# Shared value projection: eight quarter-size block products become seven, with sums of weight blocks and of activation blocks made beside them

## The chip, the cores and the metric

The kernel runs on one core of a Trainium2 chip. The metric is the device time of one execution in microseconds (us); the time before is 1315.62 us, the median of three runs (1315.57 to 1315.96).

## What is computed

The reference chains two small transformer blocks over 512 tokens of width 1024 in float32. The change touches one product in the first block, the shared values that every head of a later attention layer reads:

```python
if i == N_A - 1:
    kv = rmsnorm(x, kv_ln_g) @ w_kv_shared
    k_sh = kv[..., :MIX_WIDTH].reshape(B, S, N_HEADS, HEAD_DIM).transpose(0, 2, 1, 3)
    v_sh = kv[..., MIX_WIDTH:].reshape(B, S, N_HEADS, HEAD_DIM).transpose(0, 2, 1, 3)
```

Here `x` is 512 x 1024 and each half of `w_kv_shared` is 1024 x 1024. The keys' half is computed by the stage `sh_k`, the values' half by the stage `sh_v`.

## The kernel before

All programs of the five engines are written out by hand, one instruction list per engine; semaphores order them. The work is a list `LINEARS` of matrix products that TensorE walks one after the other. The stages that matter here are, in order, `gate0`, `sh_k`, `sh_v`, `sb_gate`.

Each product is made in float32 by splitting: every operand has a high part (rounded to `F32R`) and a low part (what is left), and each 128 x 128 by 128 x 512 product is three matmuls, high x high, high x low, low x high (`three`, L494 to L498). A weight matrix is read in **slabs** of two 128-row tiles by 512 columns (128 partitions x 1024 numbers, 512 KB):

- SyncE (SP) loads the slab into one of four `stage` buffers (`load`, L465), once VectorE has finished with the slab four places before (`lo_ready`);
- ScalarE (ACT) writes its high part to one of two `w_hi` buffers (`split` of ACT, L1108), once TensorE has finished with the slab two places before (`ring_used`);
- VectorE (DVE) writes the low part to `w_lo` (`split` of DVE, L1689), and that is what TensorE waits for (`lo_ready`).

One slab serves 24 matmuls: two k-tiles, four output tiles, three products each. A group of 512 output columns is four slabs and fills four of the eight PSUM banks; the next group uses the other four. A stage of 1024 columns is two groups, eight slabs, 192 matmuls.

While TensorE works on a stage, ACT and DVE do other things in between the slabs: `linear(name, read, extra)` walks the slabs in order; at each slab it first calls `split_to`, then reads finished banks, then pops one entry of the list `extra`. So an entry of `extra` stands behind the split of one slab and ahead of the split of the next on that engine. During `sh_k` the entries are the split of the next activations (`hi_two`, `lo_two`) and, on DVE, the RMS norm's tail (`norm`, L1770 to L1781).

The norm of this layer is finished inside `sh_k`: before its matmuls of k = 6, TensorE sums the squares over the tokens' features (`token_sums`, L592); DVE and POOL make the reciprocal root; at k = 7 TensorE spreads it (L605, `rstd_done`). `sh_k` multiplies it in when its banks are read (`kT_sh`, L1795). `sh_v` is computed with tokens on the partitions, so its banks are scaled by one number per partition (`nrm`) when ACT copies them to `v_sh` (L1194). POOL has nothing to do during `sh_v` except clearing two buffers.

The buffers: `stage`, `w_hi`, `w_lo` as above; `xT` holds the layer's input, `a0h`/`a0l` the high and low part of the gained activations, `s_...` and `sv_slot` appear only in the change.

Of the kernel before, what the change touches and what calls it, by code (L numbers as in the profile page):

```python
# [114 lines left out]
def build(nc, ctx, ins, out, cols):  # L115
# [90 lines left out]
    rope_b = [put(f"rope_b{s}", [P, MB, ROPE], 84.5 + 0.5 * s) for s in range(2)]  # L206

    kT_sh = put("kT_sh", [P, KD, T], 32)
    v_sh = put("v_sh", [P, MB, D], 48)
# [133 lines left out]
    def columns(a, b, step=T):  # L343
# [15 lines left out]
        Linear("sh_k", w_sh, 8, columns(0, D), False, A0, items("h_kv")),  # L359
        Linear("sh_v", w_sh, 8, columns(D, 2 * D), True, A0, items("h_kv")),  # L360
        Linear("sb_gate", w_sb, 8, columns(D, 2 * D), False, A1, items("h_sb")),
# [17 lines left out]
    read_by = {"out0a": ("src_ready", source(first_item["x0"]) - 1), "out0": ("src_ready", source(first_item["x0"]) + 3), "out1": ("src_ready", source(first_item["x1"]) - 1),  # L379
               "g_out": ("x_new", 24), "b_out": ("x_new", 32),  # L380
               "gate1": ("g_read", 0), "g_v": ("g_read", 8), "g_u": ("g_read", 24), "g_g": ("g_read", 40)}
    bank_free = {"mla_gate0": [("mla_cq_read", 4), ("src_ready", source(first_item["latent"] + 4))], "mla_gate1": [("mla_gate1_read", 7)] * 2}
    group_read = []
    for L in LINEARS:
        lin[L.name] = L
        L.load0, L.group0 = len(loads), n_groups
        L.read, L.read0 = read_by.get(L.name, (L.name + "_read", 0))
        for g, (c0, w) in enumerate(L.groups):
            group_read.append((L.read, L.read0 + 4 * (g + 1)))
            if L.by_tile:  # L390
                for c in range(c0, c0 + w, P):
                    loads.append((L, 0, L.kt, c, P))
            elif L.name == "out0a":
                loads.append((L, 0, 6, c0, P))
                for k0 in range(0, 6, 2):
                    loads.append((L, k0, 2, c0 + P, w - P))
                loads.append((L, 6, 2, c0, w))
                L.lpg = 5
            else:
                for k0 in range(0, L.kt, 2):  # L400
                    loads.append((L, k0, min(2, L.kt - k0), c0, w))
        n_groups += L.n
# [17 lines left out]
    def end_load(name):  # L420
        return lin[name].load0 + lin[name].lpg * lin[name].n

    def slab(t, L, nk, w):
# [5 lines left out]
    loaded = [S(f"loaded{s}") for s in range(4)]  # L429
    block = ctx.enter_context(nc.Block())  # L430
# [19 lines left out]
    def _(sp_):  # L450
# [3 lines left out]
        def load(r, i=None):  # L454
            L, k0, nk, c0, w = loads[r]
            src = L.w[k0 * P:(k0 + nk) * P, :].rearrange("(k p) n -> p k n", p=P)
            turn = 0 if i is None else i * (2 * L.lpg)
            if r >= 4:
                sp_.wait_ge(S("lo_ready"), turn + (r - 3))
# [5 lines left out]
            sp_.dma_start(slab(stage[r % 4], L, nk, w), src).then_inc(loaded[r % 4], 16)  # L465

        for r in range(end_load("proj0")):
            load(r)
        for m in range(MB):
            sp_.dma_start(x_tok[:, m, :], ins["x"][0, m * P:(m + 1) * P, :]).then_inc(S(f"x_in{m}"), 16)  # L470
        for L in LINEARS[1:]:
            if L.name in LOOPED:
                with sp_.Fori(0, L.n // 2) as i:
                    for r in range(L.load0, L.load0 + 2 * L.lpg):
                        load(r, i)
            else:
                for r in range(L.load0, end_load(L.name)):
# [15 lines left out]
    def _(pe):  # L493
# [130 lines left out]
        def x_columns(a, b):  # L624


            def do():
                if a == 0:
                    pe.wait_ge(S("gains_ok"), 2)
                    pe.wait_ge(S("act_lo"), 2)  # L630
                    for m in range(MB):
                        pe.wait_ge(S(f"x_in{m}"), 16)
                for k in range(a, b):
# [184 lines left out]
        linear("sh_k", 1)  # L818
        linear("sh_v")
        linear("sb_gate")  # L820
# [261 lines left out]
    def _(act):  # L1082
# [10 lines left out]
        def split(r, i=None):  # L1093
# [5 lines left out]
            if r == 0:  # L1099
# [4 lines left out]
                return  # L1104
            act.wait_ge(loaded[r % 4], 16 * (r // 4 + 1) + turn * 32)
            if r >= 2:
                act.wait_ge(S("ring_used"), r - 1 + turn * 8)
            act.activation(slab(w_hi[r % 2], L, nk, w), slab(stage[r % 4], L, nk, w), ACT.Copy).then_inc(S("hi_ready"), 1)  # L1108

# [359 lines left out]
        def sb_values(i, first=False):  # L1469
            if not first:  # L1470
                act.wait_ge(S("o2_done"), 2 * i)
            vs = v_sh[:, :, i * P:(i + 1) * P] if isinstance(i, int) else v_sh[:, :, bass.ds(i * P, P)]
            act.activation(v_pair2[:, :, :], vs, ACT.Copy).then_inc(S("v2_ok"), 1)
# [192 lines left out]
    def _(dve):  # L1666
# [10 lines left out]
        def split(r, i=None):  # L1677
# [4 lines left out]
            if r == 0:  # L1682
# [5 lines left out]
            dve.wait_ge(S("hi_ready"), r + 1 + (0 if i is None else 8 * i))  # L1688
            dve.tensor_tensor(slab(w_lo[r % 2], L, nk, w), slab(stage[r % 4], L, nk, w), slab(w_hi[r % 2], L, nk, w), ALU.subtract)\  # L1689
               .then_inc(S("lo_ready"), 1)  # L1690
# [18 lines left out]

        def linear(name, read=None, extra=(), then=None, first=None, further=False, near=False):  # L1710

# [12 lines left out]
            def groups(count, i=None):  # L1724
# [9 lines left out]
                if first:  # L1734
                    first()
                reads(count - 1, range(2), i)
                if further:
# [336 lines left out]
        rest_of_layer(0, 1, "h_kv")  # L2074
        linear("sh_k", normed_to(kT_sh, 1), [nothing, nothing, norm(1, 1e-6, "sh_k")] + [lo_two("h_sb", t) for t in range(4)])
        linear("sh_v")
        linear("sb_gate", normed_to(sg, 1))
# [290 lines left out]
    def _(pool):  # L2368
# [7 lines left out]

        pool.wait_ge(S("x_in3"), 16)
        for w, name in enumerate(("mla_q_head_g", "mla_k_head_g")):
# [101 lines left out]

        root(nrm, MB, "nrm_in", 2, "nrm_ok")
        pool.wait_ge(S("x_new"), 16)
        def kq_parts(pair, s, kq):
# [14 lines left out]

        pool.wait_ge(S("sh_k_read"), 8)
        def no_low(t, s):  # L2500

# [159 lines left out]
```

## Time and profile before

| what | value |
|---|---|
| median of three runs | 1315.62 us (1315.57 to 1315.96) |
| span of the profiled execution, first to last instruction | 1314.1 us |
| TensorE busy | 1295.6 us, 99% of the span |
| VectorE, ScalarE, GpSimd busy | 758.1, 642.3, 343.7 us |
| TensorE's share of the chain that ended last | 89% |
| `sh_v` on TensorE | 384.73 to 428.25 us |

The span is the part of an execution that the trace covers; the 1.5 us between it and the median lie around it and are not in the trace. The chain that ended last is followed back from the last instruction to what released each step, so an engine's share there is time that it, and not a wait, set.

### The profile page before, as it was taken

How to read it: one execution, taken by the hardware profiler on the slowest of the kernel's cores; microseconds unless marked ns; L12 is line 12 of the kernel's file. 1: busy time of each engine (PE TensorE's matmuls, PEld its weight loads, DVE VectorE, ACT ScalarE, POOL GpSimd, SP SyncE). 2: the span in 40 equal slices, each digit the busy share in tenths (PEclk: the TensorE clock that was granted, in tenths of full speed). 3: DMA queues.
4: the chain of work that ended last, by engine and by line, in shares of the span. 5: the costliest groups of instructions: out<-in, count | busy, mean ns of one | idle time of the engine just before them, and what ended most of it. 6: DMA issues, size and time to landing. Idle time of an engine off the chain costs nothing.

```text
span 1314.1 us, 17855 instructions
## 1 busy us (share of the span) xinstructions
PE 1295.6 (99%) x6478; PEld 1086.5 (83%) x6478; DVE 758.1 (58%) x1209; ACT 642.3 (49%) x1164; POOL 343.7 (26%) x393
## 2 busy tenths in 40 slices
PE   7999999999999999999999999999999999999998
PEld 6998778788888888888888888889888888888986
DVE  5656889735652226898444653335467335578843
ACT  5379888624432325998244433414234234355632
POOL 2238877400000007773000000000000000668620
PEclk9999999999999999999999999999999999999999
DMA  5332100132232232001323333332332421421121
GB/s 192 84 108 65 45 25 15 53 106 97 81 99 97 99 99 73 17 0 32 112 97 93 87 93 97 96 97 64 87 110 82 135 96 49 129 65 49 33 64 65
DMA packets 70867, 104.66 MB, mean 80 GB/s; under 512 B 3476, under 2 KB 31368, under 8 KB 70664
## 3 DMA queue, kind: packets, MB, share of 16 engines
q1 hardware_dynamic: 69584, 99.44, 24.3%
q0 software_dynamic: 1088, 4.17, 1.1%
q8 instruction: 47, 0.77, 0.2%
q14 instruction: 28, 0.23, 0.1%
q10 hardware_dynamic: 120, 0.05, 0.0%
HBM read 101.55 MB, written 2.10 MB: 79 GB/s over the span
## 4 chain that ended last, share of the span: by engine, by line
PE 89%; DVE 5%; issue 3%; ACT 2%; DMA 1%; SPq 0%; DVEq 0%; POOL 0%; ACTq 0%; POOLq 0%
PE ps L496 24%; PE ps L498 23%; PE ps L497 23%; PE ps L700 3%; PE ps L1006 2%; PE ps L858 2%; PE ps L713 1%; PE ps L950 1%; PE ps L679 1%; PE ps L727 1%; PE ps L848 1%; DVE sp L2086 1%; PE ps L849 1%; PE ps L728 1%; DVE sp_l L2091 1%
## 5 line engine op out<-in xcount | busy, mean ns | idle before, releaser
L1689 DVE TENSOR_TENSOR w_lo<-stage,w_hi 128x1024 fp32r<-128x1024 f32 (+4 forms) x188 | 224.1, 1192 | 415.1 <-ACT w_hi L1108 414.9
L1108 ACT ACTIVATE w_hi<-stage 128x1024 fp32r<-128x1024 f32 (+4 forms) x188 | 191.0, 1016 | 457.2 <-PE ps L498 456.8
L496 PE MATMUL ps<-a0h,w_hi 128*128 128x512 f32 x512 | 204.5, 399 | 1.1 <-DVE q_lo L2273 0.8
L498 PE MATMUL ps<-a0h,w_lo 128*128 128x512 f32 x512 | 199.9, 390 | 0.0
L497 PE MATMUL ps<-a0l,w_hi 128*128 128x512 f32 x512 | 199.5, 390 | 0.0
L2375 POOL TENSOR_TENSOR small<-small 128x16 f32<-128x16 f32 (+2 forms) x14 | 32.3, 2311 | 388.0 <-DVE small L1767 284.4
L496 PE MATMUL ps<-w_hi,a0h 128*128 128x512 f32 (+1 forms) x320 | 121.9, 381 | 0.1
L498 PE MATMUL ps<-w_hi,a0l 128*128 128x512 f32 (+1 forms) x320 | 119.9, 375 | 0.0
L497 PE MATMUL ps<-w_lo,a0h 128*128 128x512 f32 (+1 forms) x320 | 119.8, 374 | 0.0
L496 PEld LDWEIGHTS ps<-a0h,w_hi 128*128 128x128 f32 x512 | 96.2, 188 | 20.5 <-DVE w_lo L1689 1.3
L498 PEld LDWEIGHTS ps<-a0h,w_lo 128*128 128x128 f32 x512 | 96.1, 188 | 20.6
L497 PEld LDWEIGHTS ps<-a0l,w_hi 128*128 128x128 f32 x512 | 96.3, 188 | 18.2 <-issue 0.2
L496 PE MATMUL ps<-a1h,w_hi 128*128 128x512 f32 x256 | 99.9, 390 | 0.3 <-DVE w_lo L1689 0.3
L498 PE MATMUL ps<-a1h,w_lo 128*128 128x512 f32 x256 | 99.6, 389 | 0.0
L497 PE MATMUL ps<-a1l,w_hi 128*128 128x512 f32 x256 | 99.6, 389 | 0.0
L496 PEld LDWEIGHTS ps<-w_hi,a0h 128*128 128x128 f32 x320 | 60.1, 188 | 11.6 <-issue 0.9
L497 PEld LDWEIGHTS ps<-w_lo,a0h 128*128 128x128 f32 x320 | 60.1, 188 | 10.5 <-issue 0.7
L498 PEld LDWEIGHTS ps<-w_hi,a0l 128*128 128x128 f32 x320 | 60.1, 188 | 10.2
L496 PEld LDWEIGHTS ps<-a1h,w_hi 128*128 128x128 f32 x256 | 48.1, 188 | 10.7 <-DVE w_lo L1689 0.7
L498 PEld LDWEIGHTS ps<-a1h,w_lo 128*128 128x128 f32 x256 | 48.1, 188 | 10.1
L497 PEld LDWEIGHTS ps<-a1l,w_hi 128*128 128x128 f32 x256 | 48.1, 188 | 9.8
L496 PE MATMUL ps<-yh,w_hi 128*128 128x512 f32 x128 | 49.9, 390 | 0.0
(330 smaller groups left out, 2840.0 us busy)
## 6 DMA issues: line engine op xcount, KB each, us to landing
stage<-in_a_w_in SPq DMA_DIRECT2D x48, 512.0 KB, 3.7
stage<-in_ple_w_gate SPq DMA_DIRECT2D x16, 512.0 KB, 3.3
stage<-in_w_kv_shared SPq DMA_DIRECT2D x16, 512.0 KB, 3.6
stage<-in_sb_w_in SPq DMA_DIRECT2D x16, 512.0 KB, 3.7
stage<-in_a_w_out SPq DMA_DIRECT2D x16, 512.0 KB, 3.4
stage<-in_b_w_in SPq DMA_DIRECT2D x16, 512.0 KB, 3.7
stage<-in_mla_w_in SPq DMA_DIRECT2D x8, 512.0 KB, 3.9
stage<-in_sb_w_out SPq DMA_DIRECT2D x8, 512.0 KB, 3.4
```

The lines of the kernel that those rows point to most:

```text
L496: pe.matmul(bank, wh, mh, start=start and not seeded, stop=False, skip_group_check=seeded)
L497: pe.matmul(bank, wh, ml, start=False, stop=False, skip_group_check=seeded)
L498: return pe.matmul(bank, wl, mh, start=False, stop=stop, skip_group_check=seeded)
L679: t = pe.transpose(ps[bank][0:QK, m * P:(m + 1) * P], ring[s][:, m, :], ident)
L700: pe.matmul(ps[b][:, c:c + n], qT[s][0:QK, j * P:(j + 1) * P], kT[s][0:QK, 0:n], start=j != 0, stop=False, skip_group_check=True)
L713: t = pe.transpose(ps[3 + b][:, c + (q - j) * P:c + (q - j + 1) * P], pr[:, QRY_COL[q] + j * P:QRY_COL[q] + (j + 1) * P], ident)
L727: pe.matmul(ps[6][:, j * P:T], v_hl[h % 2][:, j, :], prT_h[:, at], start=j == 0, stop=False, skip_group_check=True)
L858: t = pe.matmul(ps[6 + s][:, j * P:T], v_pair2[:, j, :], a_T[s][:, KEY_COL[j]:KEY_COL[j] + T - j * P], start=j == 0, stop=j == MB - 1, ski ...
L1006: t = pe.matmul(ps[W_OUT][:, j * P:j * P + n], v_dup[:, e, j, :], pwT[s][:, j, 0:n], start=j == 0, stop=j == MB - 1, skip_group_check=True)
L1108: act.activation(slab(w_hi[r % 2], L, nk, w), slab(stage[r % 4], L, nk, w), ACT.Copy).then_inc(S("hi_ready"), 1)
L1689: dve.tensor_tensor(slab(w_lo[r % 2], L, nk, w), slab(stage[r % 4], L, nk, w), slab(w_hi[r % 2], L, nk, w), ALU.subtract)\
L2375: return pool.tensor_tensor(ap, ap, minus_half[:, 0:n], ALU.pow).then_inc(S(ready), 1)
```

## The change

`sh_v` is no longer eight slabs but 28 **half steps**. Tokens, features and output columns are each cut in two, and the four blocks of the result are made from seven products of quarter size, where the plain way takes eight. With A11 the first 256 tokens and first four k-tiles, A22 the last of both, and B11, B12, B21, B22 the weight blocks of 512 x 512, the seven are, in the order of TensorE and by the four pairs of banks a, b, c, d:

1. a = A11 B11
2. c = (A21 - A22) t1, with t1 = B11 + B12
3. b = (A21 - A22 - A11) t2, with t2 = t1 + B22
4. d = (A11 - A21) t3, with t3 = B12 + B22
5. a is added to: A12 B21
6. c is added to: (A12 + A21 - A22 - A11) B22
7. d is added to: A22 t4, with t4 = t2 + B21

A product is four half steps of one k-tile (128 x 512 of weights) by two token tiles: 6 matmuls each. `w_hi` and `w_lo` then hold four half slots.

- **Activation sums:** during `sh_k`, ACT writes four quarter blocks of gained activations to `s_f` (16 instructions of 128 x 256, `gained`), DVE makes four sums (128 x 1024), ACT and DVE split them (`sums_hi`, `sums_lo`).
- **Weight sums:** SP loads B11 and B12 a second time into four new buffers `sv_slot` once `rstd_done` is 2, and POOL adds B12 and B22 to them with four accumulating DMAs of 512 KB (`weight_sums`) when all four loads have landed; nothing is used before all four adds have landed (`adds_in` at 64). t2 and t4 are made in place by four additions on DVE.
- **Read-out:** a bank pair is read more than once: ACT writes six copies, DVE twelve scaled additions into `v_sh` (`add`).
- TensorE waits for `first_out` at 4 ahead of product 5 and for `sums_out` at 8 ahead of product 6.
- The last bank reads of `sh_k` on DVE alternate with the first half splits (`between`). The four semaphores of the input load become one.

```diff
+class Fast:
+    SPLITS = ("b11", "t1", "t2", "t3", "b21", "b22", "t4")
+    N = 4 * len(SPLITS)
...
+            L.fast.order = []
+            for name in ("b11", "t", "b12", "b22", "b21"):
...
+            for j in range(Fast.N):
+                ring_need[L.load0 + j] = L.load0 + (j - 3 if j >= 4 else j // 2 - 1)
+            ring_need[L.load0 + Fast.N] = L.load0 + Fast.N - 2
...
+        def load_fast(L):
+            for name, p, to, src, landed, need in L.fast.order:
+                if need:
+                    sp_.wait_ge(S("lo_ready"), need)
+                if name == "t" and p == 0:
+                    sp_.wait_ge(S("rstd_done"), 2)
+                sp_.dma_start(to[:, :, :], src).then_inc(S("sums_in") if name in ("t", "b12") else landed[0], 16)
...
+            for n, (to, a) in enumerate(steps):
+                if n == 1:
+                    pe.wait_ge(S(group_read[G - 1][0]), group_read[G - 1][1])
+                    pe.wait_ge(S("s_lo"), 1)
+                if n == 2:
+                    pe.wait_ge(S("s_lo"), 4)
+                if n == 4:
+                    pe.wait_ge(S("first_out"), 4)
+                if n == 5:
+                    pe.wait_ge(S("sums_out"), 8)
+                for k in range(4):
+                    r = L.load0 + 4 * n + k
+                    pe.wait_ge(S("lo_ready"), r + 1)
...
+        def gained(sets, name):
+            def do():
+                for q in sets:
+                    k0, t0 = ((4, T // 2), (0, T // 2), (0, 0), (4, 0))[q]
+                    for k in range(4):
+                        last = act.activation(s_f[:, q, k, :], xT[:, k0 + k, t0:t0 + T // 2], ACT.Identity, scale=gain(name, k0 + k))
+                    last.then_inc(S("s_hi"), 1)
+            return do
...
-        linear("sh_k", None, [nothing] * 3 + [hi_two("h_sb", t) for t in range(4)])
-        linear("sh_v", normed_rows(v_sh, 1))
+        linear("sh_k", None, [nothing, gained((0, 1), "h_kv"), gained((2, 3), "h_kv")] + [hi_two("h_sb", t) for t in range(3)]
+               + [lambda: (sums_hi((0, 1))(), hi_two("h_sb", 3)()), sums_hi((2, 3))])
+        fast_tokens(lin["sh_v"], v_sh)
...
+            def add(to, bank, m, other, sem, op=ALU.add):
+                dve.scalar_tensor_tensor(to, bank[:, :], nrm[:, m:m + 1], other, ALU.mult, op).then_inc(S(sem), 1)
...
+            for j in range(Fast.N):
+                split_to(L.load0 + j)
+                if j in (5, 7):
+                    weight_sum((j - 5) // 2, "b22")
+                if j in (17, 19):
+                    weight_sum((j - 17) // 2, "b21")
...
+                if j == 19:
+                    dve.wait_ge(S("ring_used"), L.load0 + 16)
+                    dve.wait_ge(S(done), 2)
+                    for m in range(2):
+                        add(t[:, 2 + m, two], d[m], 2 + m, t[:, 2 + m, one], done)
+                if j == 20:
+                    dve.wait_ge(S(done), 6)
+                    for m in range(2):
+                        add(t[:, 2 + m, two], c[m], 2 + m, t[:, 2 + m, two], done, ALU.subtract)
...
+        def weight_sums(L):
+            pool.wait_ge(S("sums_in"), 64)
+            for to, a, c0 in (("t", 0, 1), ("b12", 4, 1)):
+                for p in range(2):
+                    r0, c = a + 2 * p, L.groups[c0][0]
+                    src = L.w[r0 * P:(r0 + 2) * P, c:c + T].rearrange("(k p) n -> p k n", p=P)
+                    pool.dma_start(L.fast.home[to, p][:, :, :], src, accum_op=ALU.add).then_inc(S("adds_in"), 16)
```

**First place: ACT at the turn from `gate0` to `sh_k`.** `sq` is the last square of the norm, `w_hi_51<-stage_58` is the split of `sh_k`'s fourth slab, which TensorE needs for k = 6, and `a1h` is `hi_two`. Before:

```order
L1116 ACTIVATE a0h<-xT,gains 128x512 [waits x_new]
L1175 ACTIVATE sq_66<-xT 128x512 [waits acc_done,x_new]
L1108 ACTIVATE w_hi_51<-stage_58 128x1024 [waits ring_used,loaded2]
L1108 ACTIVATE w_hi_52<-stage_59 128x1024 [waits ring_used,loaded3]
L1116 ACTIVATE a1h<-xT,gains 128x512 [waits x_new] x2
```

and with the change:

```order
L1231 ACTIVATE a0h<-xT,gains 128x512 [waits x_new]
L1290 ACTIVATE sq_66<-xT 128x512 [waits acc_done,x_new]
L1564 ACTIVATE s_f<-xT,gains 128x256 x8
L1223 ACTIVATE w_hi_51<-stage_58 128x1024 [waits ring_used,loaded2]
L1564 ACTIVATE s_f<-xT,gains 128x256 x8
L1223 ACTIVATE w_hi_52<-stage_59 128x1024 [waits ring_used,loaded3]
L1231 ACTIVATE a1h<-xT,gains 128x512 [waits x_new] x2
```

Eight instructions now stand ahead of the fourth slab's split, and eight more ahead of the fifth's.

**Second place: DVE in the middle of `sh_v`**, from the split of half step 15 (`w_lo_53<-sv_slot_123`, the second of the x2 row) to that of half step 20 and the two subtractions behind it, for which TensorE waits ahead of product 6:

```order
L1845 TENSOR_TENSOR w_lo_53<-sv_slot_123,w_hi_51 128x512 [waits hi_ready] x2
L2263 SCALAR_TENSOR_TENSOR v_sh<-ps,small,v_sh 128x512 [waits first_out,ring_used]
L2263 SCALAR_TENSOR_TENSOR v_sh<-ps,small,v_sh 128x512
L1845 TENSOR_TENSOR w_lo_54<-stage_59,w_hi_52 128x512 [waits hi_ready]
L2263 SCALAR_TENSOR_TENSOR v_sh<-ps,small,v_sh 128x512 x2
L1845 TENSOR_TENSOR w_lo_54<-stage_59,w_hi_52 128x512 [waits hi_ready]
L2274 TENSOR_TENSOR sv_slot_124<-sv_slot_124,stage_59 128x1024 [waits lo_ready,s_ok]
L1845 TENSOR_TENSOR w_lo_53<-stage_56,w_hi_51 128x512 [waits hi_ready] x2
L2274 TENSOR_TENSOR sv_slot_125<-sv_slot_125,stage_56 128x1024 [waits lo_ready,s_ok]
L2263 SCALAR_TENSOR_TENSOR v_sh<-ps,small,v_sh 128x512 [waits sums_out,ring_used]
...
L1845 TENSOR_TENSOR w_lo_54<-stage_57,w_hi_52 128x512 [waits hi_ready]
L2263 SCALAR_TENSOR_TENSOR v_sh<-ps,small,v_sh 128x512 [waits sums_out]
```

Before, DVE had in `sh_v` nothing but one low split per slab; all of these rows but the splits are new there.

## Rows read from the trace of the kernel before

**Rows 1.** The page: shares of the engines, and the chain that ended last

```profile
PE 1295.6 (99%) x6478; PEld 1086.5 (83%) x6478; DVE 758.1 (58%) x1209; ACT 642.3 (49%) x1164; POOL 343.7 (26%) x393
PE 89%; DVE 5%; issue 3%; ACT 2%; DMA 1%; SPq 0%; DVEq 0%; POOL 0%; ACTq 0%; POOLq 0%
```

**Rows 2.** Timeline of PE, start and duration: first matmuls of sh_v, first of sb_gate

```profile
384.73 0.39 PE L496 MATMUL ps<-w_hi,a0h 128*128 128x512 f32 x1
384.96 0.39 PE L497 MATMUL ps<-w_lo,a0h 128*128 128x512 f32 x1
...
428.25 0.39 PE L496 MATMUL ps<-a1h,w_hi 128*128 128x512 f32 x1
```

**Rows 3.** Timeline of ACT, start and duration: last square, sh_k's fourth and fifth slab

```profile
352.53 0.62 ACT L1175 ACTIVATE sq<-xT 128x512 f32<-128x512 f32 x1
353.06 1.04 ACT L1108 ACTIVATE w_hi<-stage 128x1024 fp32r<-128x1024 f32 x1
355.62 1.06 ACT L1108 ACTIVATE w_hi<-stage 128x1024 fp32r<-128x1024 f32 x1 [1.52 <-PE ps L498]
356.59 1.32 ACT L1116 ACTIVATE a1h<-xT,gains 128x512 fp32r<-128x512 f32 x2
```

**Rows 4.** Timeline of DVE: the same two slabs' low splits, the norm between them

```profile
354.32 1.22 DVE L1689 TENSOR_TENSOR w_lo<-stage,w_hi 128x1024 fp32r<-128x1024 f32 x1
356.68 0.16 DVE L1767 TENSOR_SCALAR small<-ps 128x4 f32<-128x4 f32 x1 [1.15 <-PE ps L592]
360.41 0.69 DVE L1780 COPY rstd<-ps 128x512 f32<-128x512 f32 x1 [1.48 <-PE ps L605]
361.02 1.22 DVE L1689 TENSOR_TENSOR w_lo<-stage,w_hi 128x1024 fp32r<-128x1024 f32 x1
```

**Rows 5.** Waits from 339 to 430 us: total, times, longest; the one that held PE

```profile
PEld ps L592 <- DVE w_lo L1689: 0.5, 1, 0.5
```

**Rows 6.** Groups of ACT by form: busy, mean ns of one

```profile
L1116 ACT ACTIVATE a1h<-xT,gains 128x512 fp32r<-128x512 f32 x16 | 10.4, 708 | 0.0
L1119 ACT ACTIVATE a1h<-xT 128x512 fp32r<-128x512 f32 x16 | 9.6, 633 | 12.8 <-DVE xT L2040 6.4 <-DVE xT L2022 6.4
L1353 ACT ACTIVATE v_hl<-kv_tok 128x256 fp32r<-128x256 f32 x8 | 3.2, 405 | 0.0
```

**Rows 7.** Groups of DVE by form: busy, mean ns of one

```profile
L1689 DVE TENSOR_TENSOR w_lo<-stage,w_hi 128x1024 fp32r<-128x1024 f32 x164 | 203.8, 1243 | 398.0 <-ACT w_hi L1108 397.8
L1700 DVE TENSOR_TENSOR cql<-tmp,cqh 128x512 fp32r<-128x512 f32 x5 | 3.4, 690 | 0.2
L2347 DVE SCALAR_TENSOR_TENSOR out_tok<-ps,small,gain_row 128x512 f32<-128x512 f32 x4 | 2.9, 745 | 0.0
```

**Rows 8.** Timeline of DVE: the low splits of sh_k's sixth and seventh slab

```profile
364.32 1.23 DVE L1689 TENSOR_TENSOR w_lo<-stage,w_hi 128x1024 fp32r<-128x1024 f32 x1 [0.76 <-ACT w_hi L1108]
369.76 1.23 DVE L1689 TENSOR_TENSOR w_lo<-stage,w_hi 128x1024 fp32r<-128x1024 f32 x1 [1.69 <-ACT w_hi L1108]
```

**Rows 9.** DMA issues: engine, count, KB each, median us from issue to landing

```profile
stage<-in_w_kv_shared SPq DMA_DIRECT2D x16, 512.0 KB, 3.6
ws_tok<-in_a_ws POOLq DMA_DIRECT2D x1, 1024.0 KB, 7.0
p_tok<-in_p POOLq DMA_DIRECT2D x1, 512.0 KB, 4.3
bq_all<-in_b_bq POOLq DMA_DIRECT2D x1, 512.0 KB, 3.9
```

**Rows 10.** Stretches of 2 us at the kernel's start, many loads queued; last column GB/s

```profile
8.00:10.00 2.00, 1.34 (x3) 1.15 (x4) 1.90 (x5) 1.86 (x3) 0.00 (x0) 1.00 1.02 418
12.00:14.00 2.00, 1.41 (x6) 0.80 (x4) 0.00 (x0) 0.00 (x0) 0.00 (x0) 1.00 1.03 385
```

More of the change, by code:

```diff
@@ L206, in build @@
     rope_b = [put(f"rope_b{s}", [P, MB, ROPE], 84.5 + 0.5 * s) for s in range(2)]
+    s_f = put("s_f", [P, 4, 4, T // 2], 64)
+    s_lo = put("s_lo", [P, 4, 4, T // 2], 64, F32R)
+    s_hi = put("s_hi", [P, 4, 4, T // 2], 0, F32R, of=SG)
+    sv_slots = [nc.alloc_sbuf_tensor_at(f"sv_slot{s}", [P, 2, T], F32, offset=SGM - 4096 + 4096 * s) for s in range(3)] \
+        + [put("sv_slot3", [P, 2, T], 80)]
     kT_sh = put("kT_sh", [P, KD, T], 32)
@@ L383, in build @@
     group_read = []
+    stage_free, ring_need, stage_of, n_stage = [0] * 4, {}, {}, 0
+    loaded = [S(f"loaded{s}") for s in range(4)]
     for L in LINEARS:
@@ L389, in build @@
             group_read.append((L.read, L.read0 + 4 * (g + 1)))
-            if L.by_tile:
+            if L.fast:
+                L.lpg = Fast.N // 2
+                loads += [(L, g * L.lpg + j, 1, c0, w) for j in range(L.lpg)]
+            elif L.by_tile:
                 for c in range(c0, c0 + w, P):
@@ L475, in _ @@
                         load(r, i)
+            elif L.fast:
+                load_fast(L)
             else:
@@ L1104, in split @@
                 return
[L1105 removed]
+            if L.fast:
+                src, name, p = L.fast.source(k0)
+                if name in ("t2", "t4"):
+                    act.wait_ge(S("s_ok"), {"t2": 5, "t4": 7}[name] + p)
+                else:
+                    act.wait_ge(*L.fast.landed[{"t1": "t", "t3": "b12"}.get(name, name), p])
+                act.wait_ge(S("ring_used"), ring_need[r])
+                act.activation(half_slot(w_hi, r), src, ACT.Copy).then_inc(S("hi_ready"), 1)
+                return
+            q, count, _ = stage_of[r]
+            act.wait_ge(loaded[q], 16 * count + turn * 32)
             if r >= 2:
[L1107 to L1108 removed]
+                act.wait_ge(S("ring_used"), ring_need.get(r, r - 1) + turn * 8)
+            act.activation(slab(w_hi[r % 2], L, nk, w), slab(stage[q], L, nk, w), ACT.Copy).then_inc(S("hi_ready"), 1)
         def hi(s):
@@ L1708, in group_done, with linear @@
             dve.wait_ge(S("ring_used"), L.load0 + (g + 1) * L.lpg + (0 if i is None else i * 2 * L.lpg))
-        def linear(name, read=None, extra=(), then=None, first=None, further=False, near=False):
+        def linear(name, read=None, extra=(), then=None, first=None, further=False, near=False, between=False):
             L, extra = lin[name], list(extra)
@@ L1735, in groups @@
                     first()
+                if between:
+                    for n in range(4):
+                        reads(count - 1, [n], i)
+                        split_to(end + 2 + min(n, 1), i)
+                    return
                 reads(count - 1, range(2), i)
@@ L2074, in _, with sums_lo, do, sums @@
         rest_of_layer(0, 1, "h_kv")
-        linear("sh_k", normed_to(kT_sh, 1), [nothing, nothing, norm(1, 1e-6, "sh_k")] + [lo_two("h_sb", t) for t in range(4)])
-        linear("sh_v")
+        def sums_lo(qs):
+            def do():
+                for q in qs:
+                    dve.wait_ge(S("s_hi"), 4 + q + 1)
+                    dve.tensor_tensor(s_lo[:, q, :, :], s_f[:, q, :, :], s_hi[:, q, :, :], ALU.subtract).then_inc(S("s_lo"), 1)
+            return do
+        def sums(qs):
+            def do():
+                for q in qs:
+                    dve.wait_ge(S("s_hi"), (2, 3, 3, 4)[q])
+                    if q > 1:
+                        dve.wait_ge(S("s_ok"), q)
+                    a, b, op = ((1, 0, ALU.subtract), (2, 1, ALU.subtract), (0, 2, ALU.subtract), (3, 2, ALU.add))[q]
+                    dve.tensor_tensor(s_f[:, q, :, :], s_f[:, a, :, :], s_f[:, b, :, :], op).then_inc(S("s_ok"), 1)
+            return do
@@ L2077, in _ @@
+        linear("sh_k", normed_to(kT_sh, 1), [nothing, nothing, norm(1, 1e-6, "sh_k")] + [lambda: (lo_two("h_sb", 0)(), sums((0, 1))()), lambda: (lo_two("h_sb", 1)(), sums((2,))()), lambda: (lo_two("h_sb", 2)(), sums((3,))()),
+                  lambda: (sums_lo((0, 1))(), lo_two("h_sb", 3)()), sums_lo((2, 3))], between=True)
+        fast_tokens(lin["sh_v"], v_sh)
         linear("sb_gate", normed_to(sg, 1))
```

131 lines of the change are left out of this document (120 added, 11 removed).

## The prediction

> **What bounds the kernel now.** I read the page first, then the chain that ended last, then the timelines of the engines around the two shared projections, and last the DMA issues. TensorE is busy 99% of the span and sets 89% of the chain [rows 1], so a matmul that falls away here shortens the run by its pace, and a wait put in front of TensorE lengthens it by its length. The other engines have room on average, but the question is where in the stage they have it. In the timeline of TensorE `sh_v` runs without a gap from 384.73 to 428.25: 192 matmuls in 43.52 us, one every 0.2267 us [rows 2], although each is recorded with 0.39 us (the records overlap). A half step of 6 matmuls is 1.36 us, a slab of 24 is 5.44 us.
>
> A second place matters. At the turn from `gate0` to `sh_k` nothing is idle: ACT goes from the last square straight to the fourth slab's split [rows 3], DVE starts that slab's low part the moment it is free [rows 4], and TensorE already waits 0.5 us for it ahead of the token sums [rows 5]. It is the only wait on DVE of any length that TensorE has from 339 to 430 us.
>
> **Term 1, the saving.** Seven products of 24 matmuls are 168, 24 fewer than 192: 24 x 0.2267 = 5.44 us less.
>
> **Term 2, eight ACT instructions ahead of the fourth slab.** The first two sets of `gained` are entry two of `sh_k`'s list on ACT, so they run behind the last square and ahead of the fourth slab's split. No row has this form. A 128 x 256 copy from SBUF takes 0.405 us; the gain as scale adds 0.708 - 0.633 = 0.075 [rows 6]; in a row two instructions start 0.1 closer than their durations say (two `a1h` of 0.71 in 1.32 [rows 3]). So 0.38 to 0.39 each, 3.1 us for eight. The split then starts at 356.2 instead of 353.06 and ends at 357.2; DVE, free at 354.32 before [rows 4], starts at 357.25, so 2.95 us later, and TensorE, which was already waiting there, stands still for all of it. The norm behind the token sums (root, spread, copy of `rstd` [rows 4]) moves along and loses nothing more. Bounds: half of the 0.61 spacing of the 512-wide form gives 0.305 each and a stall of 2.2 us; 0.48 each without overlap gives 3.6. I take 2.95, since the 256-wide row is the same width.
>
> The second eight stand ahead of the fifth slab's split, which then ends at about 361.3. DVE turns to that slab only behind the norm, at 361.02 before [rows 4], 363.97 now: covered. The rest of the new work in `sh_k` (four sums, four low splits on DVE at 1.15 spacing, four copies on ACT) is tightest at the sixth slab: from 363.97 DVE has the fifth slab (1.15), two `lo` (1.33), two sums (2.3) and the sixth slab (1.24), which ends at 370.0. TensorE takes that slab three slabs ahead of `sh_v`, at 384.73 - 16.32 + 2.95 = 371.4. It is covered by 1.4 us; without this cover it would cost what is over.
>
> **Term 3, the accumulating DMAs.** On the SP queue the second half of B11 waits for the low part of `sh_k`'s sixth slab, and the four loads to be added to stand behind it. That low part ended at 365.55 before [rows 8]; now it ends at 370.0. So five loads of 512 KB leave from 370.0 on. With many loads queued the kernel moves 385 to 418 GB/s [rows 10], say 400, 1.3 us per load; one load alone lands after 3.6 us [rows 9], so 2.3 of that is fixed: the last lands at 370.0 + 2.3 + 6.5 = 378.8, and only then does POOL issue its four adds. TensorE enters `sh_v` at 387.7, wants half step 4 (t1) four steps later at 393.1, and ACT (0.63) and DVE (0.69) with their hand-overs need 1.45 for it: the adds have until 391.7, 12.9 us. No row shows an accumulating DMA. The low bound is that of plain loads queued deep: 4.3 for the first from POOL [rows 9] and 1.3 for each further, 8.2 us, no stall. POOL's own rows put the second 512 KB of a transfer at 7.0 - 4.3 = 2.7 [rows 9]: 4.3 + 3 x 2.7 = 12.4. The high bound doubles all data time, as each add must read its target too: 1.6 fixed + 8 x 2.7 = 23.2 us, a stall of 10.3. I take POOL's rate, the nearest row, and add 1.3 for a B22 load that SP issues behind the seventh slab [rows 8] into the same stretch: 13.7 us, a stall of 0.8.
>
> The Trainium skill, Collectives: The Full Stack, "The bandwidth ceiling: the fold count and why AG ≠ RS ≠ AR", says that a DMA which adds needs two source reads for one write and so delivers half of a copy's rate. By it, as an estimate, a queued add takes 2.6 instead of 1.3 us, the four 4.3 + 1.3 + 3 x 2.6 = 13.4, and the sum below would be lower by 0.3; the trace of before has nothing to test it on.
>
> **Term 4, DVE in the middle of `sh_v`.** TensorE waits ahead of product 6 for eight read-outs, the last behind half step 20's split. The half slots are four deep, so DVE can't start half step 15's low part before TensorE ends step 11; from there the list is short to follow: ACT's split and DVE's low part of step 15 (1.4 with hand-overs), then five low parts of 128 x 512 (0.69, spaced 0.61), eight scaled reads of a bank (0.745 for the same form, spaced 0.66) and two weight sums (as a 128 x 1024 low part, 1.24, spaced 1.15) [rows 7]: 1.4 + 3.05 + 5.3 + 2.3 = 12.1 us with the last one's end. TensorE needs 8 x 1.36 = 10.88 for steps 12 to 19, of which 0.16 has passed when the last record of step 11 ends. The stall is 1.4 us. Bounds: 0.9 if the reads are spaced as the low parts, 1.9 if each hand-over costs 0.05 more. Behind product 6 DVE catches up. At the end the first slab of `sb_gate` has TensorE's last two half steps (2.7 us) for its 1.06 and 1.24 [rows 3, 7] and hand-overs of 0.2: covered, by little. The first-pair copies on ACT (four of 0.6) lie in a stretch where three half slots are full.
>
> What costs nothing: POOL waits, then issues; its next work is two clearings that the trace has 100 us ahead of their use. The single input semaphore releases TensorE when all four loads are in, as the four in a row did.
>
> **Sum.** -5.44 + 2.95 + 0.8 + 1.4 = -0.3 us: the profiled span of 1314.1 becomes 1313.8, and with the 1.5 us around it the median goes from 1315.6 to 1315.3.
>
> **The rivals.**
>
> *The adds come late (slower).* One mechanism: the four accumulating DMAs need more than 16.6 us (under 126 GB/s for 2.1 MB), so t1 is over 3.7 us late and TensorE stands at half step 4. For it: they are 2.1 MB of read and write by an engine whose single rows are slower than SP's, issued only when all loads have landed; t1's first half waits for all four adds. Against it: only the two B22 loads share the DMA engines with them. At 20 us the stall is 7.1 and the time 1315.6 - 5.44 + 2.95 + 1.4 + 7.1 = 1321.6; at the high bound 1324.9. Chance 0.30.
>
> *The saving comes through (faster).* If the s_f instructions are as short as the lower bound or run while DVE still sums squares, and DVE's read-outs fit, -5.44 + 2.2 + 0.5 = -2.7 or better, 1310.2 to 1312.9. For it: both stalls rest on spacings of forms that the trace lacks. Against it: the fourth slab has no slack at all in the trace, and either term alone takes it back. Chance 0.14.
>
> *My case:* the saving is eaten by three waits that the change brings with it, with the adds landing between the low bound (no stall, 1314.5) and 16.6 us. Chance 0.56.
>
> **Numbers.** Two medians of this kernel can be told apart by about 0.2%, 2.6 us. My case lies within that: same 0.56, slower 0.30, faster 0.14. Its own range is 1313.2 (all terms at their lower bounds: -5.44 + 2.2 + 0 + 0.9 = -2.3) to 1318. The range for 8 in 10 must reach into the late adds, which at 21 us are at about 1323; what is left out is the faster case and the slowest adds.
>
> **What would show it.** In the trace after: 168 matmuls for `sh_v`; a wait of about 3 us of TensorE at the token sums, released by the fourth slab's low part, behind eight `s_f` instructions of ACT with 0.39 spacing; the accumulating DMAs issued at about 379 and the split of `sv_slot` on ACT waiting for them until about 392; a wait of about 1.4 us ahead of product 6 on DVE's `v_sh`. I am wrong if the wait at half step 4 is over 4 us, or if the token sums don't wait.

## The result: slower by 0.7%, outside the predicted range

The changed kernel takes 1324.75 us (median of four runs, 1323.69 to 1327.52) beside 1315.59 us for the kernel before (four runs, 1315.45 to 1315.96): 1.0072 times as long, with a 95% interval of 1.006 to 1.0084. Predicted were 1315.3 us and a range up to about 1323. The profiled execution took 1323.82 us, 0.9 less than the median, and spans 1322.0 us, so 1.8 us lie around its span.

The page of the changed kernel, the same two lines as [rows 1]:

```profile
PE 1294.0 (98%) x6454; PEld 1083.9 (82%) x6454; DVE 787.9 (60%) x1253; ACT 660.2 (50%) x1202; POOL 349.1 (26%) x397
PE 87%; DVE 5%; DMA 2%; issue 2%; ACT 2%; SPq 0%; POOL 0%; DVEq 0%; ACTq 0%; POOLq 0%
```

TensorE executes 24 matmuls fewer, as planned, and yet its share of the chain falls from 89% to 87%, while DMA's rises from 1% to 2%: something that moves data is now waited for. TensorE's own waits from 339 to 460 us (line, what released it, total, times, longest), where before there was the single one of 0.5 us [rows 5]:

```profile
PE ps L566 <- DVE w_lo L1845: 5.6, 1, 5.6
PE ps L662 <- DVE w_lo L1847: 3.1, 1, 3.1
PE ps L566 <- DVE v_sh L2263: 1.2, 1, 1.2
```

The timeline of TensorE shows where they stand (start, duration, operation; in brackets the idle time ahead and its releaser): the token sums, the spread of the norm behind them, the first matmul of `sh_v`, of product 2, of product 6, and of `sb_gate`.

```profile
358.43 1.05 PE L662 MATMUL ps<-ones,acc 128*128 128x1 f32 x8 [3.07 <-DVE w_lo L1847]
...
363.79 1.02 PE L675 MATMUL ps<-sq,ones 128*128 128x512 f32 x2
...
389.17 0.39 PE L566 MATMUL ps<-w_hi,a0h 128*128 128x512 f32 x1
...
400.35 0.76 PE L566 MATMUL ps<-w_hi,s_hi 128*128 128x512 f32 x1 [5.58 <-DVE w_lo L1845]
...
425.41 0.50 PE L566 MATMUL ps<-w_hi,s_hi 128*128 128x512 f32 x1 [1.18 <-DVE v_sh L2263]
...
436.55 0.47 PE L566 MATMUL ps<-a1h,w_hi 128*128 128x512 f32 x1
```

`sb_gate` starts at 436.55 instead of 428.25 [rows 2], 8.30 us later; the stretch ahead of the turn ran 0.17 earlier (ACT's last square at 352.36 instead of 352.53 [rows 3]), so 8.47 us have to be found. In the kernel before, the token sums and the spread stand here:

```profile
355.59 1.05 PE L592 MATMUL ps<-ones,acc 128*128 128x1 f32 x8
...
359.35 1.02 PE L605 MATMUL ps<-sq,ones 128*128 128x512 f32 x2
```

Going through the stages in order finds the 8.47 us:

| step | working | us |
|---|---|---|
| 24 matmuls fewer | 24 x 0.2267 | -5.44 |
| wait at the token sums | 358.43 - (355.59 - 0.17) | +3.0 |
| from token sums to the spread | 5.36, before 3.76 (359.35 - 355.59) | +1.6 |
| wait at half step 4 | due at 389.17 + 4 x 1.36 = 394.61, starts at 400.35 | +5.74 |
| the 16 half steps from there | last matmul ends its slot at 424.07; at pace 400.35 + 21.76 = 422.11 | +1.96 |
| wait ahead of product 6 | 425.41 - 424.07 | +1.34 |
| products 6 and 7 to the first matmul of `sb_gate` | 436.55 - 425.41 less 8 x 1.36 | +0.26 |
| sum | | +8.46 |

Two of the larger rows aren't waits. Behind the first two waits TensorE has all it needs and goes slower; the stretches of TensorE's busy time tell why (stretch, length, busy time and count, granted clock, DMA share, GB/s):

```profile
358.00:360.00 2.00, 1.57 (x11) 0.99 0.20 55
360.00:362.00 2.00, 2.00 (x7) 0.50 0.58 207
362.00:364.00 2.00, 2.00 (x7) 0.66 0.00 0
364.00:368.00 4.00, 4.00 (x17) 1.00 0.04 9
394.00:397.00 3.00, 0.77 (x4) 1.00 1.10 259
397.00:398.00 1.00, 0.00 (x0) 0.75 1.05 342
398.00:402.00 4.00, 1.65 (x4) 0.50 0.12 45
402.00:404.00 2.00, 2.00 (x6) 0.50 0.00 0
404.00:405.00 1.00, 1.00 (x5) 0.84 0.00 0
```

The granted clock falls from 1.00 (2.4 GHz) to 0.50 (1.2 GHz) after TensorE has stood still, and stays there for some time after it works again. It doesn't fall at a fixed place in the wait: where TensorE starts again behind the first (358 to 360) it is still 0.99, and behind the second it is down before TensorE starts (0.75 in 397 to 398). At 0.50 the matmuls of `sh_k` start at 360.28, 360.71 and 361.13, one every 0.43 us, where the pace of before is one every 0.2267.

What the two long waits hang on is in the other engines' timelines. On ACT, the first two rows are the eight `s_f` instructions and the fourth slab's split behind them; the third is the first split of t1:

```profile
352.88 3.29 ACT L1564 ACTIVATE s_f<-xT,gains 128x256 f32<-128x256 f32 x8
356.08 1.04 ACT L1223 ACTIVATE w_hi<-stage 128x1024 fp32r<-128x1024 f32 x1
...
398.85 2.19 ACT L1217 ACTIVATE w_hi<-sv_slot 128x512 fp32r<-128x512 f32 x4 [8.27 <-DMA sv_slot<-in_w_kv_shared]
```

ACT waits 8.27 us for a DMA into `sv_slot`. The four accumulating DMAs in the timeline of POOL, and in that of SP the four loads they add to, with the loads of `stage` queued behind:

```profile
381.96 5.01 POOL L2727 DMA_DIRECT2D sv_slot<-in_w_kv_shared  x4 [21.09 <-DMA sv_slot<-in_w_kv_shared]
```

```profile
371.84 2.18 SPq L533 DMA_DIRECT2D sv_slot<-in_w_kv_shared  x4
376.22 16.16 SPq L533 DMA_DIRECT2D stage<-in_w_kv_shared  x4
```

POOL is released at 381.96, issues for 5 us, and ACT goes on at 398.85: the adds take 16.9 us. Beside them the DMA engines carry loads of B22 and B21, which SP issues ahead of their use; their share is 1.05 to 1.10 in the stretches 394 to 398 above, so by this measure they are full. The DMA view of 340 to 450 us (queue: packets, MB, share of 16 engines; then an issue group with count, size and median us to landing):

```profile
q0 software_dynamic: 1088, 2.10, 11.2%
...
sv_slot<-in_w_kv_shared POOLq DMA_DIRECT2D x4, 512.0 KB, 10.1
```

### The profile page after: what moved, and what is told of

Read it like the earlier page. It is cut to its first block, busy times and chain, and to the rows that moved or that the text cites. A ratio compares the mean times of both kernels' runs of the same rounds, so it can differ in the third digit from the quotient of the medians.

```text
span 1322.0 us, 17925 instructions
## 1 busy us (share of the span) xinstructions
PE 1294.0 (98%) x6454; PEld 1083.9 (82%) x6454; DVE 787.9 (60%) x1253; ACT 660.2 (50%) x1202; POOL 349.1 (26%) x397
## 4 chain that ended last, share of the span: by engine, by line
PE 87%; DVE 5%; DMA 2%; issue 2%; ACT 2%; SPq 0%; POOL 0%; DVEq 0%; ACTq 0%; POOLq 0%
PE ps L566 23%; PE ps L568 23%; PE ps L567 23%; PE ps L769 3%; PE ps L1111 2%; DMA sv_slot<-in_w_kv_shared 2%; PE ps L963 2%; PE ps L782 1%; PE ps L953 1%; PE ps L1055 1%; PE ps L748 1%; PE ps L954 1%; PE ps L796 1%; DVE sp L2322 1%; PE ps L797 1%
## 5 line engine op out<-in xcount | busy, mean ns | idle before, releaser
L1847 DVE TENSOR_TENSOR w_lo<-stage,w_hi 128x1024 fp32r<-128x1024 f32 (+4 forms) x180 | 214.4, 1191 | 376.7 <-ACT w_hi L1223 376.5
L1223 ACT ACTIVATE w_hi<-stage 128x1024 fp32r<-128x1024 f32 (+4 forms) x180 | 182.5, 1014 | 421.6 <-PE ps L568 421.1
L566 PE MATMUL ps<-w_hi,a0h 128*128 128x512 f32 (+1 forms) x280 | 106.3, 380 | 0.1
L568 PE MATMUL ps<-w_hi,a0l 128*128 128x512 f32 (+1 forms) x280 | 104.3, 373 | 0.0
L567 PE MATMUL ps<-w_lo,a0h 128*128 128x512 f32 (+1 forms) x280 | 104.3, 372 | 0.0
L566 PEld LDWEIGHTS ps<-w_hi,a0h 128*128 128x128 f32 x280 | 52.6, 188 | 10.1 <-issue 0.9
L567 PEld LDWEIGHTS ps<-w_lo,a0h 128*128 128x128 f32 x280 | 52.6, 188 | 9.0 <-issue 0.7
L568 PEld LDWEIGHTS ps<-w_hi,a0l 128*128 128x128 f32 x280 | 52.6, 188 | 8.5
```

The costliest lines, as they stand in the source:

```text
L566: pe.matmul(bank, wh, mh, start=start and not seeded, stop=False, skip_group_check=seeded)
L567: pe.matmul(bank, wh, ml, start=False, stop=False, skip_group_check=seeded)
L568: return pe.matmul(bank, wl, mh, start=False, stop=stop, skip_group_check=seeded)
L1223: act.activation(slab(w_hi[r % 2], L, nk, w), slab(stage[q], L, nk, w), ACT.Copy).then_inc(S("hi_ready"), 1)
L1847: dve.tensor_tensor(slab(w_lo[r % 2], L, nk, w), slab(stage[stage_of[r][0]], L, nk, w), slab(w_hi[r % 2], L, nk, w), ALU.subtract)\
```

## The experiments

The first four were timed on one chip beside the kernel before at 1315.80 us (25 runs, 1314.99 to 1316.66), the other four on another beside 1315.74 us (15 runs, 1315.4 to 1317.69). The changed kernel's 1324.75 us is that of the section above; its four runs lie 3.8 us apart, so by estimate the differences to it are good to about 1 us. The theory: two waits, at the token sums (from the `s_f` list) and at half step 4 (from the adds), and a loss of clock behind each, cost more than the saving. Rivals: the extra traffic or DVE's longer list as such costs the time; the adds are late only because they start late; the adds are late only because other loads run beside them; the slow matmuls behind the waits are slow for another reason than the clock.

**1. The gained blocks later.** ACT's `s_f` instructions move from entries two and three of `sh_k`'s list to entry four, all sixteen together, behind one `hi_two`.

```diff
-        linear("sh_k", None, [nothing, gained((0, 1), "h_kv"), gained((2, 3), "h_kv")] + [hi_two("h_sb", t) for t in range(3)]
+        linear("sh_k", None, [nothing] * 3 + [lambda: (hi_two("h_sb", 0)(), gained((0, 1, 2, 3), "h_kv")())] + [hi_two("h_sb", t) for t in (1, 2)]
```

> The changed kernel with one move: the sixteen s_f instructions of ACT run behind the split of sh_k's fifth slab instead of ahead of the fourth's and the fifth's. Theory (three waits plus what the lower clock after a wait costs): the 3.1 us wait at the token sums goes back to about 0.5 us and the clock stays at full there, so 3.0 + 1.6 = 4.6 us less, about 1320.1 us; the wait at half step 4 stays at 5 to 6 us, because the low part of the sixth slab, behind which the loads stand, moves forward as far as TensorE does. Rival (the early wait is only a part of the late one: the adds end when they end, and a TensorE that comes earlier waits there longer): wait at half step 4 of about 10 us, time about 1324.7 us.

Measured: 1320.02 us (1318.4 to 1320.73), 1.0031 [1.002, 1.0042]. TensorE's waits from 339 to 460 us:

```profile
PE ps L566 <- DVE w_lo L1845: 5.7, 1, 5.7
PE ps L566 <- DVE v_sh L2263: 1.2, 1, 1.2
```

The wait at the token sums is gone and the other two are as they were. The run is 4.7 us shorter than the changed kernel: 3.0 of it is the wait, so some 1.7 came back behind it, close to what the table has for the step to the spread (1.6).

**2. The loads to be added to go first.** SP loads them ahead of B11's.

```diff
-            for name in ("b11", "t", "b12", "b22", "b21"):
+            for name in ("t", "b12", "b11", "b22", "b21"):
```

> The changed kernel with one move in SP's queue: the four loads that are added to go out ahead of B11's two, so they wait for the norm's spread (about 364.8 us) and no longer for the low part of sh_k's sixth slab (371.4 us). Theory (the adds take 15 to 17 us and are only issued too late): all adds have landed at about 390, ahead of 393.2 us, no wait at half step 4 and no low clock behind it: 5.7 + 2.0 = 7.7 us less, about 1317.0 us. Rival (POOL and its queue set the adds' end, by being slow beside DVE's work of this stretch): the adds end at 395 or later still, 2 to 6 us of the wait stay, 1319 to 1323 us.

Measured: 1317.09 us (1315.68 to 1317.82), 1.0012 [1.0002, 1.0021]. POOL's adds and TensorE's waits:

```profile
373.57 5.01 POOL L2727 DMA_DIRECT2D sv_slot<-in_w_kv_shared  x4 [12.77 <-DMA sv_slot<-in_w_kv_shared]
```

```profile
PE ps L662 <- DVE w_lo L1847: 3.1, 1, 3.1
PE ps L566 <- DVE v_sh L2263: 1.2, 1, 1.2
```

POOL is released 8.4 us earlier than in the changed kernel, and no wait stands at half step 4. That takes off 7.7 us, as forecast from the 5.7 of the wait and the 2.0 behind it. ACT still waits 1.28 us for the adds and splits t1 at 391.57, 18.0 us after the issue; the half steps that TensorE has ahead of it cover that.

**3. No weight sums by DMA.** POOL's four adds are left out and t1 and t3 are used as loaded, so the values computed are not the reference's.

```diff
-                        to, landed, need = L.fast.extra[p + 2 * (name == "t")], (S("adds_in"), 64), None
+                        to, landed, need = L.fast.extra[p + 2 * (name == "t")], (S("sums_in"), 64), None
...
-        weight_sums(lin["sh_v"])
```

> The changed kernel without the four accumulating DMAs: t1 and t3 are taken as loaded, so the two weight sums are left out of the computation. Theory: everything that the adds cost is the wait at half step 4 and the clock behind it, 7.7 us, so about 1317.0 us, with the waits of 3.1 us at the token sums and 1.2 to 1.4 us ahead of product 6 as they are. Rival (the loads themselves are late, the adds only stand in the same stretch): a wait of some us at half step 4 stays, over 1319 us.

Measured: 1317.43 us (1315.66 to 1317.83), 1.0008 [0.9999, 1.0018], as with the loads first. Once the adds are in time, that they are there costs nothing that can be measured; traffic as such isn't the cause. The profiled execution here took 1317.69 us, that of experiment 2 1315.68; their token sums and spreads show where they differ. Here:

```profile
358.31 1.55 PE L662 MATMUL ps<-ones,acc 128*128 128x1 f32 x8 [3.07 <-DVE w_lo L1847]
365.00 1.28 PE L675 MATMUL ps<-sq,ones 128*128 128x512 f32 x2
```

and in experiment 2:

```profile
358.15 1.26 PE L662 MATMUL ps<-ones,acc 128*128 128x1 f32 x8 [3.07 <-DVE w_lo L1847]
363.50 1.02 PE L675 MATMUL ps<-sq,ones 128*128 128x512 f32 x2
```

Behind the same wait of 3.07 us the step to the spread takes 6.69 us here and 5.35 there (before: 3.76). The length of the wait doesn't fix the loss behind it.

**4. Both edits, 1 and 2.**

```diff
-            for name in ("b11", "t", "b12", "b22", "b21"):
+            for name in ("t", "b12", "b11", "b22", "b21"):
...
+        linear("sh_k", None, [nothing] * 3 + [lambda: (hi_two("h_sb", 0)(), gained((0, 1, 2, 3), "h_kv")())] + [hi_two("h_sb", t) for t in (1, 2)]
```

> Both moves together: s_f behind the fifth slab's split, and the loads to be added to ahead of B11. Theory: the two waits and their clock losses go, 4.6 + 7.7 = 12.3 us less than the changed kernel, about 1312.4 us, 3.2 us below the kernel before; the wait ahead of product 6 stays. Rival (taking one wait away makes the next one longer): not under 1315 us.

Measured: 1311.43 us (1310.94 to 1311.79), 0.9965 [0.9953, 0.9978]. Of TensorE's waits only the one ahead of product 6 is left:

```profile
PE ps L566 <- DVE v_sh L2263: 1.2, 1, 1.2
```

All the new work on ACT and DVE is still there, so beyond this wait their longer lists cost TensorE nothing.

**5. DVE's two late weight sums behind its read-outs too.** Edit 4, and the two sums with B21 four half steps later (behind 21 and 23 instead of 17 and 19), so that the read-outs for product 6 come first.

```diff
-                if j in (17, 19):
-                    weight_sum((j - 17) // 2, "b21")
+                if j in (21, 23):
+                    weight_sum((j - 21) // 2, "b21")
```

> The version with both moves, and DVE's two additions for t4 moved from half steps 17 and 19 to 21 and 23, behind the two subtractions that TensorE waits for. Theory (DVE's list from half step 15 to the eighth read-out is 12.1 us long where TensorE takes 10.9; without the two additions 9.8): the wait of 1.2 us ahead of product 6 goes, about 1310.1 us. Rival (the read-outs wait for the banks, not for DVE): the wait stays, 1311.4 us.

Measured: 1309.73 us (1309.68 to 1309.84), 0.9955 [0.9942, 0.9969], the shortest of all and below the kernel before. From 339 to 460 us TensorE's matmuls wait for nobody; what is left is its weight loads' old wait at the token sums, 0.5 us as in [rows 5]:

```profile
PEld ps L662 <- DVE w_lo L1847: 0.5, 1, 0.5
```

From ACT's last square (351.96) to `sb_gate` (422.36) are 70.40 us, and before 75.72 (352.53 to 428.25): 5.32 less, the saving of 5.44 within 0.12. About 0.6 more of the 6.0 us between the medians lies ahead of that square (351.96 instead of 352.53), where of the change only the single semaphore of the input load acts; there the profiles of the kernels that all have it differ among themselves by up to 1.25 us (351.96 to 353.21), so this part isn't put down to the change.

**6. Copies in place of adds.** The same four DMAs from POOL without adding, so the sums are left out.

```diff
-                    pool.dma_start(L.fast.home[to, p][:, :, :], src, accum_op=ALU.add).then_inc(S("adds_in"), 16)
+                    pool.dma_start(L.fast.home[to, p][:, :, :], src).then_inc(S("adds_in"), 16)
```

> The changed kernel with POOL's four DMAs as plain copies into the same buffers: the two sums are left out, the bytes written, the issue on POOL and the waits are the same. Theory (an add costs the DMA engines twice a copy, because the target is read too): the four end about 6 us sooner, within 11 us instead of 16.9, so the wait at half step 4 and its low clock are gone, about 1317.1 us; their share of the 16 engines halves. Rival (POOL's issue, 5.0 us for the four, and the way from POOL set the time): still about 16 us, 1324 us.

Measured: 1316.89 us (1315.69 to 1317.5), 1.0008 [0.9999, 1.0018]. The issue on POOL, ACT's first split of t1, and the DMA view of 340 to 450 us:

```profile
381.67 2.98 POOL L2727 DMA_DIRECT2D sv_slot<-in_w_kv_shared  x4 [20.68 <-DMA sv_slot<-in_w_kv_shared]
```

```profile
391.82 1.15 ACT L1217 ACTIVATE w_hi<-sv_slot 128x512 fp32r<-128x512 f32 x2 [1.13 <-DMA sv_slot<-in_w_kv_shared]
```

```profile
q0 software_dynamic: 576, 2.10, 5.5%
...
sv_slot<-in_w_kv_shared POOLq DMA_DIRECT2D x4, 512.0 KB, 6.8
```

POOL starts them at the same time as the adds in the changed kernel (381.67 and 381.96), with the same loads on SP's queue, and TensorE doesn't wait for them: ACT goes on at 391.82, 10.1 us after the issue, in place of 16.9. So the late start alone isn't the cause; that they add is. The same 2.10 MB takes 5.5% of the sixteen engines' 110 us in place of 11.2%: 6.05 against 12.3 us, half. Copies are also issued in 2.0 us less (2.98 against 5.01); how the 6.8 us (16.9 less 10.1) divide between that and the engines' time was not tried.

The Trainium skill, Collectives: The Full Stack, "The bandwidth ceiling: the fold count and why AG ≠ RS ≠ AR", says that an adding transfer reads two sources for one write and so runs at half a copy's rate; it says so of collectives. The trace agrees for these four DMAs: 11.2% against 5.5%.

**7. B22 and B21 behind the adds.** SP holds these loads back until the adds have landed.

```diff
+                if name == "b22" and p == 0:
+                    sp_.wait_ge(S("adds_in"), 64)
```

> The changed kernel with SP's loads of B22 and B21 held until all four adds have landed, so that nothing else moves beside the adds. Theory (the three loads that now run beside them take 1.5 us of all engines each, 2 to 3 us in the adds' last stretch): the adds end within 13.5 to 14.5 us instead of 16.9, the wait at half step 4 shrinks from 5.6 to about 3 us, about 1322 us; B22 then lands at about 400, just ahead of its use. Rival (the loads cost the adds nothing): wait and time unchanged, 1324.7 us.

Measured: 1322.44 us (1322.0 to 1322.67), 1.0052 [1.0037, 1.0068]. POOL's issue and ACT's first split of t1:

```profile
381.40 5.01 POOL L2729 DMA_DIRECT2D sv_slot<-in_w_kv_shared  x4 [20.51 <-DMA sv_slot<-in_w_kv_shared]
```

```profile
396.02 2.19 ACT L1219 ACTIVATE w_hi<-sv_slot 128x512 fp32r<-128x512 f32 x4 [5.50 <-DMA sv_slot<-in_w_kv_shared]
...
401.97 0.63 ACT L1219 ACTIVATE w_hi<-sv_slot 128x512 fp32r<-128x512 f32 x1 [1.46 <-DVE sv_slot L2276]
```

With nothing beside them the adds take 14.6 us, so the other loads lengthen them by 2.3 us of 16.9. TensorE's wait at half step 4 falls from 5.6 to 2.8 us but stays:

```profile
PE ps L568 <- DVE w_lo L1847: 2.8, 1, 2.8
```

The second of ACT's rows shows a price of the edit: B22 now comes late, and with it DVE's sum t2, for which ACT waits 1.46 us; TensorE doesn't wait for that. It loses more behind the shorter wait, though: from its start on half step 4 (397.52) to the end of product 5 (422.21) it takes 2.93 us over its pace, where the changed kernel lost 1.96, with the granted clock at 0.50 from 398 to 402. So in the profiles 1.8 us come off (1323.82 to 1322.0), not 2.8. The neighbours are a part of the cause, the smaller one.

**8. Throw-away matmuls in the waits.** TensorE does 13 matmuls whose results nobody reads while it waits at the token sums, and 25 while it waits at half step 4.

```diff
+                    if L.name == "sh_k" and g == 0 and k == 6:
+                        pe.wait_ge(S(group_read[G - 1][0]), group_read[G - 1][1])
+                        for _ in range(13):
+                            pe.matmul(ps[4 * ((G + 1) % 2)][:, :], L.acts[0][0][:, 0:P], L.acts[0][0], start=True, stop=True)
...
+                    for _ in range(25):
+                        pe.matmul(there[2][:, :], L.acts[0][0][:, 0:P], L.acts[0][0], start=True, stop=True)
```

> The changed kernel with throw-away matmuls of TensorE in its two long waits, into banks that are free: 13 ahead of the token sums (2.95 us), 25 ahead of half step 4 (5.67 us). What the kernel computes is the same. Theory (behind a wait of 3 us or more the matmuls run at half clock for some 3 to 5 us, which costs 1.6 us behind the first and 2.0 us behind the second): both losses go, the waits stay as long as they are, now filled, about 1321.2 us. Rival (the low clock is only a part of the wait's own price, or comes for another reason): 1324.7 us or more.

Measured: 1320.6 us (1319.93 to 1321.06), 1.0039 [1.0023, 1.0054], 4.1 us shorter than the changed kernel with more work on TensorE. The stretches behind the two waits (columns as above):

```profile
358.00:362.00 4.00, 3.87 (x22) 1.00 0.40 131
...
398.00:402.00 4.00, 4.00 (x19) 1.00 0.00 0
402.00:406.00 4.00, 4.00 (x19) 1.00 0.00 0
```

The clock stays at 1.00, and ACT still waits 8.26 us for the adds: seen from TensorE, what these waits are for is as late as it was, only the slow matmuls behind them are gone. The step from the token sums to the spread takes 3.78 us, before 3.76:

```profile
358.17 1.05 PE L665 MATMUL ps<-ones,acc 128*128 128x1 f32 x8
...
361.95 1.02 PE L678 MATMUL ps<-sq,ones 128*128 128x512 f32 x2
```

So the slow matmuls were the clock's doing. That they need a wait of 3 us, as the theory put it, doesn't hold: experiment 7 has them behind 2.8.

## Why the prediction was wrong, by its own steps

**Term 1, the saving: right.** Experiment 5 shows 5.32 of the 5.44 us as soon as TensorE's three new waits are gone.

**Term 2, eight `s_f` instructions: right in place and size.** They took 3.29 us, 0.41 each; forecast were 3.1 and 0.39. The stall was forecast at 2.95 and came to 3.0; experiment 1 removed it by moving these eight and the eight behind them, and nothing else. The covers named for the fifth and sixth slab held: no wait of TensorE stands there.

**Term 3, the accumulating DMAs: the step that failed, in size.** The mechanism and the place were named, with 0.8 us; it came to 5.74. The forecast had the loads land at 378.8, the adds take 13.7 us, and 12.9 us to do it in. They landed at 381.96, 3.1 later. TensorE arrived at half step 4 only 1.5 later (394.61 for 393.1), so the time to do it in shrank to 11.15 us (1.5 us ahead of 394.61 for the splits). And the adds took 16.9. So 0.8 + 1.8 for the shorter time + 3.2 for the slower adds = 5.8. Of the 3.1 us of delay 1.6 is the clock behind the token sums, which slows TensorE and so frees the buffers later: with the clock kept at 1.00 (experiment 8) POOL was released at 380.35. The rest is the five loads. DVE's low part of the sixth slab, behind which they stand, ended at 371.41, 1.4 later than the 370.0 of the forecast, which is no more than the clock's part:

```profile
370.19 1.22 DVE L1847 TENSOR_TENSOR w_lo<-stage,w_hi 128x1024 fp32r<-128x1024 f32 x1
```

From there to POOL's release are 10.5 us, and the forecast had 8.8; in between, at 376.22, SP starts a load of B22 beside them, which the forecast counted only against the adds. What it costs the five loads was not tried. Of the slower adds, 2.3 us are the neighbours (experiment 7): the forecast allowed 1.3 for one B22 load where three loads ran beside them. Without neighbours the adds took 14.6 where POOL's own rate [rows 9] gave 12.4; that rate was one of a copy, and an add costs the DMA engines twice a copy (experiment 6). The nearest row was of a cheaper operation and was slower than the copies of experiment 6 (10.1 us for four, beside other loads), which hid a part of the doubling.

**Term 4, DVE ahead of product 6: right.** 1.4 us forecast, 1.34 found; experiment 5 removed it by moving the two weight sums that the term counts.

**A term that wasn't there: the clock.** The sum charged each wait with its length and put what comes behind it at nothing, without a reason. Behind the two waits of 3.1 and 5.6 us TensorE ran at half clock for a while, at 1.6 and 1.96 us more in the profiled execution; filling them with matmuls gave 4.1 us back in the medians. The wait of 1.3 us had no such cost: the granted clock is 1.00 from 424 to 436 behind it, and from 405 to 420 in experiment 4, which has that wait alone.

The forecast of no change hung on -5.44 + 2.95 + 0.8 + 1.4. With the adds at their measured size it would have been 4.9 higher, with the clock another 3.6, and products 6 and 7 with `sb_gate`'s first slab, taken as covered, added 0.26. This is the rival "the adds come late", with 16.9 us just over the 16.6 that it named, plus the later start and the clock: at 16.9 us alone it would have given 1318.5, and 1324.75 came. The condition for being wrong, a wait of over 4 us at half step 4, was met. Some of its sums are off by 0.1 to 0.2 (the high bound adds up to 1324.8 instead of 1324.9, the bounds of term 2 to 2.3 and 3.7 instead of 2.2 and 3.6, the top of its own range to 1318.2); nothing rests on that.

## What to carry to other kernels

Ask of each new transfer what releases it and what it runs beside, and cost one that adds at twice the engines' time of a copy: here four adds of 512 KB needed 14.6 us undisturbed and 16.9 beside three loads, and what stood ahead of them on SP's queue decided whether TensorE saw that. A saving on the engine that bounds the kernel is worth its full size only if every list that feeds it keeps the work due next at its front; moving sixteen instructions on ACT, four loads on SP and two sums on DVE turned the same arithmetic from 1324.75 to 1309.73 us. A wait of TensorE of 3 us here cost 4.6, one of 5.7 cost 7.7, and one of 2.8 (experiment 7) some 5.9, so such a wait is priced with the slow matmuls behind it.

## What the runs showed of the hardware

The length of a wait doesn't fix the loss of clock behind it. In the profiles with the wait of 3.07 us at the token sums, the step to the spread took 5.25 us (experiment 6), 5.36 (the changed kernel) and 6.69 (experiment 3), in place of 3.76; at half step 4, 2.93 us were lost behind a wait of 2.8 us (experiment 7) and 1.96 behind one of 5.6. The loss seems to vary between executions of one program as well. The times of experiment 3 fall into two groups, three runs at 1315.66 to 1315.99 and seven at 1317.12 to 1317.83, with a mean granted clock of 0.998 in the first and 0.997 in the second; those of experiment 6, with the same wait, lie between 1315.69 and 1317.5 without such a gap; experiments 4 and 5, which have no such wait, spread over 0.85 and 0.16 us. Of the kernel before, one run of 15 (1317.69) has 0.997 too, so its clock can fall as well. What decides how much an execution loses was not tried.

An accumulating DMA also costs its issuer more: four took POOL 5.01 us to issue, and four copies of the same shape 2.98 us; the DMA view counts 1088 packets in the adds' queue and 576 in the copies', for the same 2.10 MB.
